# One inference step of a hybrid decoder layer: the first gather of the expert stage, and what is issued around it, put in another order

## The reference

```python
h = rms_norm(x, g_pre) * (1 + sc1) + sh1
out = mixer(h) @ w_out                        # recurrent branch and attention
x = x + gt1 * rms_norm(out, g_mix_post)
h = rms_norm(x, g_ffn_pre) * (1 + sc2) + sh2
logits = h @ w_router + b_router              # 32 experts, the top 4 of each row
# expert e, for the rows that chose it:
gu = xb @ w_gate_up[e] + b_gate_up[e]         # (rows, 1024) @ (1024, 2048)
act = x_glu * sigmoid(1.702 * x_glu) * (x_lin + 1)      # clamped
y = act @ w_down[e] + b_down[e]               # weighted, summed into the rows
x = x + gt2 * rms_norm(y, g_ffn_post)
```

## Time and profile before

| | us |
|---|---|
| median of 3 runs | 1434.68 |
| lowest and highest of them | 1430.50, 1436.26 |
| the profiled execution, its own time | 1436.92 |
| its span from the first to the last instruction | 1435.1 |
| mean granted TensorE clock, as a share of full speed | 0.972 |
| PE busy | 1355.4 (94% of the span) |
| DVE busy, ACT busy | 337.9, 224.7 |
| DMA | 486.81 MB, mean 339 GB/s |

### The profile page before, as it was taken

One profiled execution on the slowest core, in us unless ns is written; L12 is line 12 of the kernel. 1 busy time (PEld: TensorE's weight loads), 2 busy tenths in 40 slices (PEclk: granted clock), 3 DMA queues, 4 the chain that ended last, 5 costly groups with the idle time before them and its releaser, 6 DMA issues.

```text
span 1435.1 us, 15755 instructions
## 1 busy us (share of the span) xinstructions
PE 1355.4 (94%) x6279; PEld 623.1 (43%) x6279; DVE 337.9 (24%) x711; ACT 224.7 (16%) x448; POOL 25.5 (2%) x56
## 2 busy tenths in 40 slices
PE   6999999999789999999999999999999989999996
PEld 3566666664464343333333334334343333433432
DVE  2543324342433111110210102201121011220123
ACT  1113304332422110010110101101011010110102
POOL 1100000010001000000000000000000000000000
PEclk9999999999877999999999999999999999999998
DMA  9746485432548499999999999999999999999992
GB/s 349 253 155 262 162 288 166 165 108 77 168 137 351 193 417 428 427 422 428 427 427 427 419 429 427 429 426 424 428 425 428 428 422 418 424 427 428 428 427 93
DMA packets 63258, 486.81 MB, mean 339 GB/s; under 512 B 10349, under 2 KB 15205, under 8 KB 35540
## 3 DMA queue, kind: packets, MB, share of 16 engines
q1 hardware_dynamic: 61508, 480.85, 81.5%
q0 software_dynamic: 1680, 4.91, 1.0%
HBM read 481.63 MB, written 4.12 MB: 338 GB/s over the span
## 4 chain that ended last, share of the span: by engine, by line
PE 74%; DMA 20%; DVE 2%; ACT 1%; issue 1%; SPq 1%; DVEq 0%; ACTq 0%
PE bank L1734 34%; DMA ring<-in_w_gate_up_dram 20%; PE bank L1389 10%; PE bank L1411 5%; PE bank L1699 4%; PE bank L1274 4%; PE bank L1722 3%; PE bank L1700 2%; PE bank L1568 2%; PE bank L1341 2%; PE bank L1525 1%; PE bank L1295 1%; DMA ring<-in_w_ada_dram 1%; PE bank L1500 1%; PE bank L1636 1%
## 5 line engine op out<-in xcount | busy, mean ns | idle before, releaser
L1734 PE MATMUL bank<-ring,work 128*64 128x512 f32 x2048 | 459.0, 601 | 16.6 <-issue 10.7
L1734 PEld LDWEIGHTS bank<-ring,work 128*64 128x64 f32 x2048 | 161.2, 138 | 292.5 <-issue 292.1
L1734 PE MATMUL bank<-ring,hT 128*64 128x512 f32 x1024 | 232.2, 599 | 15.7 <-DMA ring<-in_w_gate_up_dram 15.7
L1251 DVE TENSOR_TENSOR gbT<-gbT,bank 128x512 f32<-128x512 f32 x85 | 58.4, 687 | 455.7 <-PE bank L1722 395.1
L1734 PEld LDWEIGHTS bank<-ring,hT 128*64 128x64 f32 x1024 | 76.4, 137 | 160.4 <-issue 160.4
L1389 PE MATMUL bank<-hT,ring 128*128 128x320 f32 x512 | 142.2, 438 | 1.6 <-DVE hT L772 1.6
L1389 PEld LDWEIGHTS bank<-hT,ring 128*128 128x128 f32 x512 | 97.2, 192 | 47.4 <-issue 8.0
L1220 DVE TENSOR_SCALAR work<-bank 128x512 f32<-128x512 f32 x32 | 21.9, 686 | 319.9 <-PE bank L1734 319.9
L1411 PE MATMUL bank<-hT,ring 128*128 128x320 f32 x256 | 72.4, 436 | 0.0
L1699 PE MATMUL bank<-qT,tok 128*128 128x256 f32 x256 | 72.4, 405 | 0.0
L723 ACT ACTIVATE work<-bank 128x320 f32<-128x320 f32 x16 | 7.0, 438 | 412.9 <-PE bank L1274 412.9
(11 more groups left out here) (335 smaller groups left out, 851.9 us busy)
## 6 DMA issues: line engine op xcount, KB each, us to landing
ring<-in_w_gate_up_dram SPq DMA_DIRECT2D x128, 2048.0 KB, 14.8
ring<-in_w_down_dram SPq DMA_DIRECT2D x64, 2048.0 KB, 17.0
ring<-in_w_ada_dram SPq DMA_DIRECT2D x12, 2048.0 KB, 10.6
ring<-in_w_in_dram SPq DMA_DIRECT2D x12, 2048.0 KB, 11.0
ring<-in_cache_k_dram SPq DMA_DIRECT2D x16, 512.0 KB, 5.9
ring<-in_cache_v_dram SPq DMA_DIRECT2D x16, 512.0 KB, 4.3
ring<-in_w_out_dram SPq DMA_DIRECT2D x2, 2048.0 KB, 7.8
out_dram<-tok POOLq DMA_DIRECT2D x2, 1024.0 KB, 5.8
```

Source lines behind the costliest of these rows:

```text
L1251: TTo(piece(gbf, n), piece(gbf, n), B[6 + n % 2][:, :], ALU.add).then_inc(s["scatter_read"], 1)
L1734: last = mm(bank[CAP * x:CAP * x + CAP, :], lhsT[:, CAP * x:CAP * x + CAP], rhs(x), start=start, stop=stop)
```

## The change

It does seven things.

1. The prompt part of the first gather is issued ahead for all eight blocks, in bank order (`gather_prompt`): two blocks each at the two norm waits, one behind the transposes of the samples' normed rows, two behind the samples' router, one behind the ranks.
2. After `sel_made` 2 only the eight sample matmuls remain (`gather_sample`), in the order 0, 4, 1, 5, 2, 6, 3, 7, so that neighbours read different halves of the partitions. Each bank has one accumulation group. ScalarE's four copies follow in the order of the banks.
3. The three `G3` pieces are made in steps b = 5, 6 and 7 of the sample loop, ahead of `sfold(b)`, and copied by ScalarE there. `gain_of_sample(B[6], 2)` behind the loop now waits for `G3_made` 3.
4. The transposed weights of the first combination go to bank 7 and are copied by VectorE in two parts.
5. GpSimd no longer waits for the samples' router before it issues the four bias loads `bgu`.
6. In every pair the bias matmuls come ahead of step k = 6 and its wait for `gu_in[6]` and `gu_in[7]`, instead of behind it.
7. The five pieces of a combination go in the order 4, 0, 1, 2, 3; at the end the cross-partition sum of the sample rows waits for one square instead of five, and ScalarE loads the table of its square root before the squares.

```diff
@@ tensor block, the sample loop and behind it
                 if b == 5:
                     ranks_of_prompt()
+                    gain_of_prompt(B[6], 5, 0).then_inc(s["G3_ps"], 1)
+                if b == 6:
+                    gain_of_prompt(B[5], 5, 1).then_inc(s["G3_ps"], 1)
+                if b == 7:
+                    eng.wait_ge(s["wt_made"], 6)
+                    eng.wait_ge(s["G3_made"], 1)
+                    gain_of_sample(B[6], 5).then_inc(s["G3_ps"], 1)
                 sfold(b)
-            eng.wait_ge(s["wt_made"], 6)
+            eng.wait_ge(s["G3_made"], 3)
             gain_of_sample(B[6], 2).then_inc(s["gains_ps"], 1)
@@ the first gather
+            def first_out(m):
+                return B[GBANK[m // 2]][:, QUAD * (m % 2):QUAD * (m % 2) + QUAD]
+            def gather_prompt(m):
+                for k in range(2):
+                    mm(first_out(m), tok[:, k, 128 * m:128 * m + 128], sel[:, k, :], start=(m % 2 == 0 and k == 0), stop=False)
+            def gather_sample(m):
+                q = 64 * (m // 4)
+                return mm(first_out(m), tok[q:q + 64, 2, 128 * (m % 4):128 * (m % 4) + 128], sel[q:q + 64, 2, :],
+                          start=False, stop=(m % 2 == 1))
...
-            for m in (0, 2):
-                gather_first(m, (0, 1))
+            gather_prompt(0)
+            gather_prompt(1)
             eng.wait_ge(s["x1_sq"], 5)
             both_halves(1)
-            eng.wait_ge(s["mo_made"], 5)
-            for m in (4, 6):
-                gather_first(m, (0, 1))
+            gather_prompt(2)
+            gather_prompt(3)
...
             last.then_inc(s["h2T_ps"], 1)
+            eng.wait_ge(s["mo_made"], 5)
+            gather_prompt(4)
             eng.wait_ge(s["h2T_made"], 5)
...
             last.then_inc(s["router_ps"], 1)
-            for h in range(2):
-                gain_of_prompt(B[3 + h], 5, h).then_inc(s["G3_ps"], 1)
-            gain_of_sample(B[5], 5).then_inc(s["G3_ps"], 1)
+            gather_prompt(5)
+            gather_prompt(6)
...
+            gather_prompt(7)
             eng.wait_ge(s["sel_made"], 2)
-            for m in range(NT):
-                last = gather_first(m, (0, 1, 2) if m % 2 else (2,))
-                if m % 2:
-                    last.then_inc(s["gather_ps"], 1)
+            for m in range(4):
+                for q in (m, m + 4):
+                    last = gather_sample(q)
+                    if m % 2:
+                        last.then_inc(s["gather_ps"], 1)
@@ in pair
                         last.then_inc(s["cT_ps"], 1)
-                    if k == 6:
                         eng.wait_ge(s["esel_made"], t + 1)
                         for j in range(4):
                             both(B[j], esel[E * j:E * j + E, :], lambda x: bgu[E * j:E * j + E, :], False, False)
@@ gpsimd block
-            eng.wait_ge(s["router_ps"], 2)
             for j in range(4):
                 eng.dma_start(bgu[E * j:E * j + E, :], b_gate_up[0][:, 512 * j:512 * j + 512]).then_inc(s["bgu_in"], 16)
@@ the end of the tensor and of the scalar block
-            eng.wait_ge(s["f_sq"], NPC)
+            eng.wait_ge(s["f_sq"], 1)
...
+            A_(sst[:, 0, 0:1], ones[:, 0:1], ACT.Sqrt)
```

More of the change, by code:

```diff
@@ L688, in _ @@
                     A_(tope[:, 0:2, 0:TOPK], tope[:, 0:2, 0:TOPK], ACT.Exp).then_inc(s["topexp_made"], 1)
+                if b >= 5:
+                    eng.wait_ge(s["G3_ps"], b - 4)
+                    A_(G3(b - 5), B[5 + b % 2][:, :].rearrange("p (t n) -> p t n", t=2), ACT.Copy).then_inc(s["G3_made"], 1)
             eng.wait_ge(s["gains_ps"], 1)
@@ L701, in _ @@
             A_(tope[:, 2, 0:TOPK], tope[:, 2, 0:TOPK], ACT.Exp).then_inc(s["topexp_made"], 1)
-            eng.wait_ge(s["op_ps"], 5)
-            for i in range(3):
-                eng.wait_ge(s["G3_ps"], i + 1)
-                A_(piece(G3, i), B[3 + i][:, :], ACT.Copy).then_inc(s["G3_made"], 1)
             def XT_out(buf, half, first, bank):
@@ L737, in _ @@
             done = moe_rounds(eng, pair)
-            for i in range(NPC):
-                eng.wait_ge(s["scatter_read"], NPC * done + i + 1)
+            A_(sst[:, 0, 0:1], ones[:, 0:1], ACT.Sqrt)
+            for n, i in enumerate(SCATTER):
+                eng.wait_ge(s["scatter_read"], NPC * done + n + 1)
                 A_(piece(work[:, 2048:4608], i), piece(gbf, i), ACT.Square, accum_out=ss[:, 10 + i:11 + i]).then_inc(s["f_sq"], 1)
@@ L1192, in _ @@
             eng.wait_ge(s["moe_zeroed"], 2)
-            V_.tensor_copy(C[0:E, :], B[4][0:E, 0:T]).then_inc(s["C_made"], 1)
+            link.later(V_.tensor_copy(C[0:E, 0:SP_], B[7][0:E, SP_:2 * SP_]))
+            link(V_.tensor_copy(C[0:E, SP_:T], B[7][0:E, 0:NS]))
+            eng.sem_inc(s["C_made"], 1)
             def weigh(col):
@@ L1256, in _ @@
             eng.wait_ge(s["G3_made"], 3)
-            for n in range(NPC):
+            for n, i in enumerate(SCATTER):
                 eng.wait_ge(s["f_sq"], n + 1)
-                link.later(TTo(piece(gbf, n), piece(gbf, n), piece(G3, n if n == 1 else (0, 1, 0, 1, 2)[n]), ALU.mult))
+                v = piece(gbf, i).rearrange("p (t n) -> p t n", t=2)
+                link.later(TTo(v, v, G3(2 if i == 4 else i % 2), ALU.mult))
             halves(r3[:, 0:2], ss[:, 10:14])
@@ L1647, in _ @@
             GBANK = (0, 1, 6, 2)
-            def gather_first(m, tiles):
-                out = B[GBANK[m // 2]][:, QUAD * (m % 2):QUAD * (m % 2) + QUAD]
-                for k in tiles:
-                    q = 64 * (m // 4)
-                    if k < 2:
-                        last = mm(out, tok[:, k, 128 * m:128 * m + 128], sel[:, k, :], start=(k == 0), stop=False)
-                    else:
-                        last = mm(out, tok[q:q + 64, 2, 128 * (m % 4):128 * (m % 4) + 128], sel[q:q + 64, 2, :], start=False, stop=True)
-                return last
+            def first_out(m):
[7 more added lines that the diff above has]
+                          start=False, stop=(m % 2 == 1))
             eng.wait_ge(s["op_sq"], 5)
@@ L1704, in _ @@
             eng.wait_ge(s["wtok_made"], 2)
-            eng.wait_ge(s["G3_made"], 2)
             for k in range(TT):
-                last = tr(B[4][0:E, 128 * k:128 * k + TROWS[k]], wtok[0:TROWS[k], k, :], TROWS[k])
+                o = SP_ + 128 * k if k < 2 else 0
+                last = tr(B[7][0:E, o:o + TROWS[k]], wtok[0:TROWS[k], k, :], TROWS[k])
             last.then_inc(s["wt_ps"], 1)
@@ L1719, in combine @@
                         eng.wait_ge(s["scatter_read"], NPC * t + (n - 1))
-                    k, bank = n // 2, B[6 + n % 2]
+                    i, bank = SCATTER[n], B[6 + n % 2]
+                    k = i // 2
                     if k < 2:
-                        last = mm(bank[:, :], C[:, 128 * k:128 * k + 128], Ysb[:, 512 * (n % 2):512 * (n % 2) + 512], start=True, stop=True)
+                        last = mm(bank[:, :], C[:, 128 * k:128 * k + 128], Ysb[:, 512 * (i % 2):512 * (i % 2) + 512], start=True, stop=True)
                     else:
```

15 lines of the change are left out of this document (8 added, 7 removed).

## The result

The changed kernel takes 1423.79 us (median of 4 runs, 1422.16 to 1426.06), the kernel before 1435.47 beside it (4 runs, 1430.5 to 1436.86). The ratio is 0.9938 with an interval of 0.9911 to 0.9964, 3.6 to 8.9 thousandths faster.

The account below looks back on a forecast made before the run. The pairs were taken as bound by weight transfers, with time ahead of the first new transfer counting in full. -10.26 + 0.35 + 3.1 - 1.04 = -7.85, taken as -6.7 for a typical run: 1428.0 us, range 1424.5 to 1432.5.

Parts of the forecast that it names:

- The gather: From the samples' selection to the first pair: 3.65 us instead of 13.91, so -10.26.
- Two of the eight may run in the time of one: Sample matmuls on different partition halves may overlap: eight take between 2.1 and 4.2 us, taken as 2.4.
- The drain at a change between 128 and 64 rows: In the gather, changing tiling mode drains TensorE; the old order alternated, the new one changes once; no size given.
- The clock: In the gather TensorE was expected to stay at 2.4 GHz because four full-size prompt blocks stand in the former thin stretch.
- rival of a slow gather: TensorE at 1.2 GHz again or halves not overlapping, leaving -2.5 or -6.5 of -7.85: 1430.5 to 1434; chance 0.20.
- slower: Clock not recovered before the first pair, so a step k takes twice 3.65; all eight give 1458; chance 0.05.
- What comes ahead of it: Ahead of the gather, block 4 delays the router by 0.35 us; blocks 5, 6 and 7 add nothing.
- The gains in the loop: Sample loop steps b = 5, 6 and 7: the moved gains cost 0, 1.7 and 1.4 us, together +3.1.
- the gains cost nothing: Extra work at b = 5 to 7 raises the clock and shortens the output projection: -11, 1424 to 1427; chance 0.20.
- Bias ahead of k = 6: In the last pair the bias matmuls now lie in the wait for weights: -1.04 us.
- The others: Items 4, 5 and 7 (VectorE's copies, bias loads, combination order and end of kernel): 0 us each.
- a typical run should lie between, near -6.7: Whole kernel: between -7.85 and -5.1, the latter if the old gather ran at 2.4 GHz; 1434.68 - 6.7 = 1428.0.

Follow-up runs that it names:

- e6: The changed kernel with the first gather as before, in its old split of prompt and sample matmuls: 1435.15 us, ratio 1.0015 to the kernel before.
- e5: The changed kernel with the eight sample matmuls in the order 0 to 7, ScalarE's copies following the banks: 1424.92 us, ratio 0.995 to the kernel before.
- e9: The changed kernel with the old gather and eight dummy matmuls of prompt-block size ahead of it: 1430.51 us, ratio 0.9983 to the kernel before.
- e10: The changed kernel with prompt blocks 5, 6 and 7 issued with block 4 ahead of the samples' router: 1427.82 us, ratio 0.9968 to the kernel before.
- e2: The changed kernel with all three gains in step b = 5, behind its fold: 1422.93 us, ratio 0.9922 to the kernel before.
- e11: The changed kernel with all three gains in step b = 5, run again: 1421.75 us, ratio 0.9928 to the kernel before.
- e7: The changed kernel with the three gains moved from the loop to behind the samples' router, ahead of blocks 5 and 6: 1423.11 us, ratio 0.9934 to the kernel before.
- e1: The changed kernel again, unedited: 1423.85 us, ratio 0.9933 to the kernel before.
- e12: The changed kernel once more, unedited, in a later set: 1424.28 us, ratio 0.9947 to the kernel before.
- e8: The changed kernel with items 5 and 7 taken back: 1424.11 us, ratio 0.9932 to the kernel before.

## Why the prediction was right, and where it was off

**The gather.** Predicted -10.26, measured -10.44, and by the mechanism that was forecast. Its parts: eight matmuls 2.4 against 2.00; from the selection to the end of the last copy 3.4 against 3.22 (457.88 to 461.10); from there to the first pair 0.25, as measured. So the limit was ScalarE's copies, as the sum had it, and the 0.4 too much for the matmuls counts for 0.2 only. The prediction's other figure, a first pair 3.05 after the selection without the copies as a limit, does not follow from its 2.4 for the matmuls: 2.4 + 0.1 + 0.6 + 0.25 is 3.35. e6 shows that this item is the whole change: without it the rest is worth nothing that can be measured. "Two of the eight may run in the time of one" was right, and e5 shows it: 2.96 without alternation. The Trainium skill (TensorEngine Tiling (Array Packing), Key Properties) has tiles of the array work independently; the runs agree, 2.00 against 2.96. The drain at a change between 128 and 64 rows, which the prediction names, shows no time of its own. In e9's timeline the prompt's matmuls of 128 rows and the samples' of 64 rows alternate:

```profile
462.52 1.13 PE L1667 MATMUL bank<-qT,tok 128*128 128x256 f32 x4
463.58 1.13 PE L1669 MATMUL bank<-qT,tok 64*128 64x256 f32 x4
464.64 1.13 PE L1667 MATMUL bank<-qT,tok 128*128 128x256 f32 x4
```

Two matmuls of either kind take 1.06 from start to start.

**The clock.** The prediction counted on 2.4 GHz because dense prompt blocks stand in the thin stretch. That was an argument only. e9 and e10 support it from both sides: dense work in the gaps ahead of the old gather keeps the clock at 1.00, and three of the changed kernel's prompt blocks moved ahead of the router let it fall. Of the 10.5 us between the old gather (13.98 in e6) and the new one (3.47), 4.8 are the clock's and 5.7 the shorter program's. By the Trainium skill (TensorE: Matmul & The Clock Gate, Part 1) activity releases the clock; e9 agrees, 13 us to 8.3. The rival of a slow gather is out: every profiled execution that kept the prompt blocks and the order of the eight matmuls where the change puts them had 2.00 us for the eight. So is the rival "slower": the first step of the first pair took 3.65 in all of them, not twice that.

**What comes ahead of it.** Taken as +0.35 for block 4, measured -0.04 from the end of the output projection to the selection. The router started 7.58 behind the projection's end, 7.48 before: block 4 fills the wait for ScalarE's copy nearly to the end. That 1.2 us of idle time covers block 7 was right (e10, without it: 1.20 again).

**The gains in the loop.** Predicted +3.1, measured +3.51, by e2 too. The term that was too small is the 1.7 for one gain at 1.2 GHz, for which I gave the gap between two instructions a price that doesn't double: it took 2.00, near the upper bound of 2.1, and `svalues(7)` came 2.22 later behind S (7.17 against 4.95). From there to the output projection it was 1.29 more (7.67 against 6.38), where 1.4 was predicted, and at b = 5 nothing.

The rival "the gains cost nothing" is out as a mechanism. It supposed that they would raise the clock in the loop, and the clock at its end is 0.50 as before. The shorter output projection that it named did come, 8.70 against 9.50, but it is no effect of the gains: with all three at b = 5 it was 8.72 in e2 and 9.54 in e11, which are the same kernel, without them in the loop 9.53 in e7, with them as changed 8.7 in e1 and e12 and 9.5 in e6 and e10. It differs by execution.

**Bias ahead of k = 6.** Predicted -1.04, and "can't give more than 1.04 unless pauses of the queue shrink". From L to D it gave 1.20. The other 0.15 is the step k = 6 itself: followed by the bias it took 3.59 (1387.10 to 1390.69), followed by the next step 3.44 (7.09 less 3.65). The pauses are unsettled, as said.

**The others.** Items 5 and 7: 0 predicted, and 0 by e8. Item 4, also put at 0, has no run of its own; in the trace the first pair waits for ScalarE's copy (`ACT work L718`) and not for VectorE.

**The total.** The sum of the steps was -7.85 and the trace gives -8.56. The step that made the forecast too high came behind the sum: "a typical run should lie between, near -6.7". It supposed that in other executions the old gather ran at 2.4 GHz, and that the spread of the runs came from there. Both traces with the old gather and no fillers, of before and of e6, have 13 us and PEclk 0.50. What the traces show of the spread lies elsewhere, in the part before S (it starts at 419.8 to 427.2) and in the output projection. So nothing that was seen supports taking 1.1 us off the sum. It is not excluded for single executions: one run of e6 without a trace took 1427.89 at a mean granted clock of 0.981, where the other nine have 0.974 to 0.979. From 1434.68 the sum alone gives 1426.8. Of the 3.0 us left to the measured median, 0.7 are the difference of sum and trace; the rest is within the spread of the kernel before, whose four medians here lie between 1432.8 and 1435.5, while those of the changed kernel lie between 1423.8 and 1424.3. The changed kernel's three ratios, 0.9938, 0.9933 and 0.9947, are 8.9, 9.6 and 7.6 us, around the 8.56 of the trace and the 7.85 of the sum, and above the 6.7 of the forecast.

## What to carry to other kernels

When a short critical stretch ends a chain of small matmuls and waits, look at the granted clock inside it. Work that doesn't depend on the chain gains twice if it is moved ahead: it is off the path, and it keeps the clock up for what remains. But it has to stand within the chain's gaps: put ahead of the router in e10, 2.6 us of it lay on the path and the clock fell to 0.82. And a faster step is worth only what the step behind it lets through: 1.0 us off the eight matmuls brought the first pair 0.4, because ScalarE's copies then end last. Before a spread of run times is explained by the stage under study, compare a second execution of the same kernel from an event just ahead of that stage.

## What the runs showed of the hardware

- Two matmuls of 64 rows that read different halves of the partitions and write different banks stream at once, and by the three orders they seem to start in program order: eight of them, 256 columns of fp32 each, took 2.00 us alternating, 2.10 in twos and 2.96 one half after the other. Different banks alone don't do it: two on one half into different banks took 2.01 at 1.2 GHz, two on different halves 1.16.
- Eight dummy matmuls with a result that nobody reads made a kernel faster, 1435.15 to 1430.51, by the clock: its sixteen matmuls took 8.3 us instead of 13.
- Dense work ahead of a thin stretch didn't keep the clock: behind four dense blocks, the router, the ranks and waits of 1.83 and 1.20 us brought PEclk from 1.00 (455 to 460) to 0.82 (460 to 465, e10). With three of the blocks between them it stayed at 1.00.
- The first dense block of the program, 24 records at 17 to 18 us, takes 4.08 in some executions and 7.14 in others of the same kernel.
